# Last two key projections of dilated attention as a group of seven half-size products, two pairs of buffers for its queries and keys, and a scan begun on half of its stacks

## The reference

```python
h = rms_norm_2(x, norm_w[layer])
proj = h @ w_in[layer].astype(f32)
u_s, z_s, q, k, v, z_a, r_s, r_a = jnp.split(proj, offsets, axis=-1)
y_s = s5_branch(u_s, ...)                        # state space scan, then GLU
y_s = (y_s * jax.nn.silu(z_s)) @ w_ssm_out[layer].astype(f32)
q = apply_partial_rope(rms_norm_2(q.reshape(head_shape), q_norm_w...), positions)
k = apply_partial_rope(rms_norm_2(k.reshape(head_shape), k_norm_w...), positions)
y_a = dilated_attention(q, k, v)                 # 3 dilations, 8 heads of 64
y_a = (y_a * jax.nn.silu(z_a)) @ w_attn_out[layer].astype(f32)
m = jax.nn.sigmoid(r_s) * y_s + jax.nn.sigmoid(r_a) * y_a
x = x + m @ w_o[layer].astype(f32)
```

## Time and profile before

| what | value |
|---|---|
| three runs | 970.54, 970.54, 969.59 us, median 970.54 us |
| the profiled execution's own time | 969.14 us |
| its span, first to last instruction | 967.2 us |
| TensorE busy | 954.4 us, 99% of the span |
| VectorE busy | 697.0 us, 72% |
| ScalarE busy | 220.4 us, 23% |
| granted TensorE clock | 1.000 of full speed over the whole span |

### The profile page before, as it was taken

How to read it: one execution, slowest core, us unless ns; L and a number is a source line. 1 busy time by engine, 2 the same in 40 slices (tenths; PEclk the granted TensorE clock), 3 DMA queues, 4 the chain that set the end, 5 groups by cost and what they waited for, 6 DMA issues and landing times.

```text
span 967.2 us, 12513 instructions
## 1 busy us (share of the span) xinstructions
PE 954.4 (99%) x5014; PEld 590.6 (61%) x5014; DVE 697.0 (72%) x1259; ACT 220.4 (23%) x438; POOL 23.2 (2%) x27
## 2 busy tenths in 40 slices
PE   7999999999999999999999999999999999999998
PEld 6944445754555449999844469458854444468544
DVE  4866964586566887866899763888965969674667
ACT  4313422223241232422200011001011321434200
POOL 0000000000002500000000000000000000000000
PEclk9999999999999999999999999999999999999999
DMA  9551731443345624344454443425243434321631
GB/s 329 149 196 43 283 130 44 174 134 128 97 158 155 182 109 169 115 175 175 174 174 173 174 149 124 164 88 175 87 138 124 173 116 150 109 105 45 218 130 44
DMA packets 53818, 139.76 MB, mean 144 GB/s; under 512 B 3968, under 2 KB 7904, under 8 KB 53760
## 3 DMA queue, kind: packets, MB, share of 16 engines
q1 hardware_dynamic: 52304, 135.07, 39.7%
q0 software_dynamic: 1248, 3.80, 1.7%
q10 hardware_dynamic: 208, 0.08, 0.0%
HBM read 137.90 MB, written 1.05 MB: 144 GB/s over the span
## 4 chain that ended last, share of the span: by engine, by line
PE 92%; DVE 5%; ACT 1%; issue 1%; DMA 0%; DVEq 0%; ACTq 0%
PE pair L1947 36%; PE pair L2032 18%; PE pair L2028 16%; PE pair L2286 6%; PE turned L1892 4%; PE score L2286 3%; DVE arena L928 3%; PE turned L2286 1%; PE score L2381 1%; PE score L2457 1%; PE score L2131 1%; PE score L2444 1%; PE score L2183 1%; PE score L2130 1%; PE score L2199 1%
## 5 line engine op out<-in xcount | busy, mean ns | idle before, releaser
L1947 PE MATMUL pair<-ring,hT 128*128 128x512 f32 (+2 forms) x640 | 269.8, 576 | 0.9 <-ACT hT L600 0.9
L928 DVE TENSOR_TENSOR arena<-arena 128x512 f32<-128x512 f32 (+6 forms) x329 | 194.1, 604 | 13.4 <-PE score L2286 4.1
L1947 PEld LDWEIGHTS pair<-ring,hT 128*128 128x128 f32 x640 | 119.2, 190 | 130.5 <-issue 125.5
L1947 PE MATMUL pair<-hT,ring 128*128 128x128 f32 (+2 forms) x464 | 76.4, 324 | 0.2 <-ACT hT L600 0.2
L928 DVE TENSOR_TENSOR arena<-pair,arena 128x512 f32<-128x512 f32 x57 | 39.4, 691 | 46.6 <-PE pair L2032 22.7
L2032 PE MATMUL pair<-ring,arena 128*128 128x512 f32 x160 | 71.7, 594 | 0.0
L1947 PEld LDWEIGHTS pair<-hT,ring 128*128 128x128 f32 (+1 forms) x464 | 66.0, 188 | 9.0 <-issue 1.3
L928 DVE TENSOR_TENSOR arena<-ring 128x2048 f32<-128x2048 f32 (+1 forms) x37 | 67.7, 1831 | 2.5 <-DMA ring<-in_w_ssm_out 1.3
L2032 PE MATMUL pair<-arena 128*128 128x512 f32 x144 | 65.3, 595 | 0.3 <-DVE arena L928 0.3
L2028 PE MATMUL pair<-arena 128*128 128x128 f32 x544 | 64.0, 276 | 0.0
L2032 PE MATMUL pair<-ring,hT 128*128 128x512 f32 x136 | 62.4, 598 | 0.8 <-DMA ring<-in_w_in 0.8
(11 more groups left out here) (221 smaller groups left out, 1004.4 us busy)
## 6 DMA issues: line engine op xcount, KB each, us to landing
ring<-in_w_in SPq DMA_DIRECT2D x33, 2048.0 KB, 8.4
ring<-in_w_up SPq DMA_DIRECT2D x8, 2048.0 KB, 8.5
ring<-in_w_down SPq DMA_DIRECT2D x8, 2048.0 KB, 7.8
ring<-in_w_o SPq DMA_DIRECT2D x4, 2048.0 KB, 7.9
ring<-in_w_mem_kv SPq DMA_DIRECT2D x2, 2048.0 KB, 7.8
ring<-in_w_glu SPq DMA_DIRECT2D x2, 2048.0 KB, 7.8
ring<-in_w_ssm_out SPq DMA_DIRECT2D x2, 2048.0 KB, 7.8
ring<-in_w_ukv SPq DMA_DIRECT2D x4, 512.0 KB, 3.7
```

Source lines behind the costliest of these rows:

```text
L928: return dve.tensor_tensor(o, a, b, op)
L1947: ins = pe.matmul(o_, s, m, start=a, stop=b)
```

## The change

The blocks dk1 and dk2 become a group of seven named DK, ahead of RS. RS then shares its row sums with DK. Places for sums are moved. A second pair of buffers (`raws[1]`) is laid over memory that the scan has left; blocks alternate between the pairs. The last two blocks get one inverse root over 32 columns instead of two over 16, and their squares come from ScalarE out of SBUF after the group's results are complete. Block 5 (dk2) is turned before block 4 (dk1). Only the first eight stack copies stay on VectorE; ScalarE makes the other eight before it takes dv0. TensorE's first drive comes ahead of any quarter of the early jobs. The wait for the last transposes, which stood behind T1 of RA on VectorE, now stands ahead of it, because T1 of RA is written over a buffer that these transposes read.

```diff
@@ -81,7 +81,8 @@
 
 
 RG, MV, UP = 3, 4, 5
-RS = UP + 4
+DK = UP + 4
+RS = DK + 1
...
@@ -111,8 +112,9 @@
     j += [(f"zs{i}", "w_in_2", C_ZS + 512 * i, 512) for i in range(2)]
     j += [("za", "w_in_2", C_ZA, DW)]
     j += [(f"dq{g}", "w_in_2", C_DQ + DW * g, DW) for g in range(NDIL)]
-    j += [(f"dk{g}", "w_in_2", C_DK + DW * g, DW) for g in range(NDIL)]
+    j += [("dk0", "w_in_2", C_DK, DW)]
     out += [(n, n, w, 0, DM, c, m) for n, w, c, m in j]
+    out += halves(DK, C_DK + DW, "w_in_2")
     out += halves(RS, C_RS, "w_in_2") + halves(RA, C_RA, "w_in_2") + halves(GLU, 0, "w_glu_2")
     out += [(f"ao{i}", f"ao{i}", "w_attn_out_2", 0, DW, 512 * i, 512) for i in range(2)]
...
 
...
         assert a4.at <= work_at
+        raws = ((raw, raw2), (sig_glu[:, 0:1024], sig_glu[:, 1024:2048]))
         tail_q1, tail_q5 = arena[:, 7680:8192], arena[:, 16384:16896]
-        tail_t2 = {RS: m_tok, RA: sig_glu, GLU: m_tok, SO: arena[:, work_at:work_at + 2048], WP: arena[:, work_at + 4096:work_at + 6144]}
+        tail_t2 = {DK: arena[:, 0:2048], RS: arena[:, 2048:4096], RA: sig_glu, GLU: zs, SO: arena[:, work_at:work_at + 2048], WP: arena[:, work_at + 4096:work_at + 6144]}
         rows_raw = arena[:, work_at + 6144:work_at + 8192]
-        tail_rows = {RS: zs, RA: zs, GLU: rows_raw, SO: arena[:, work_at + 2048:work_at + 4096], WP: rows_raw}
+        tail_rows = {DK: m_tok, RS: m_tok, RA: m_tok, GLU: rows_raw, SO: arena[:, work_at + 2048:work_at + 4096], WP: rows_raw}
...
@@ -443,6 +448,18 @@
 
             t, g = n // 2, 2 * (i - UP) + n % 2
             return hup[:, 1024 * g:1024 * g + 1024].rearrange("p (k t) -> p k t", t=SEQ)[:, :, P * t:P * t + P]
+
+        def stacks(i):
+
+            u4 = uT.rearrange("p (m c s) -> p m c s", c=CH, s=2)
+            v4 = u2.rearrange("p (m h c) -> p m h c", h=2, c=CH)
+            out_ = []
+            for h in range(2):
+                for jj in range(2):
+                    for s in range(2):
+                        q, r = 64 * h + 32 * jj, 64 * jj + 32 * s
+                        out_.append((h, jj, s, u4[q:q + 32, 4 * i:4 * i + 4, :, s], v4[r:r + 32, 4 * i:4 * i + 4, h, :]))
+            return out_
 
         block = ctx.enter_context(nc.Block())
...
@@ -816,6 +833,10 @@
                     if t == 0:
                         ins.then_inc(sem("u_ready"), 1)
                 ins.then_inc(sem("taken_act"), 1)
+            act.wait_ge(sem("taken_act"), taken("us1")[1])
+            for h, jj, s, src, dst in stacks(1):
+                ins = act.activation(dst, src, ACT.Copy)
+            ins.then_inc(sem("u2_late"), 1)
...
-                if n:
-                    for _k in range(2):
-                        turned((qdT if n - 1 < 3 else kdT)[:, 1024 * ((n - 1) % 3) + 512 * _k:1024 * ((n - 1) % 3) + 512 * _k + 512], 512)
-                if n == 0:
-                    act.wait_ge(sem("h_ready"), 4 * 8)
+            def turned_dqk(n):
+
+                for k in range(2):
+                    turned((qdT if n < 3 else kdT)[:, 1024 * (n % 3) + 512 * k:1024 * (n % 3) + 512 * k + 512], 512)
+
+            act.wait_ge(sem("z_silu"), 3)
+            act.wait_ge(sem("h_ready"), 4 * 8)
+            for n, name in enumerate(("dq0", "dq1", "dq2", "dk0")):
+                x, squares = raws[n % 2]
                 p = arrived(name)
                 for t in range(2):
-                    act.activation(raw[:, 512 * t:512 * t + 512], p[:, 512 * t:512 * t + 512], ACT.Copy)
+                    act.activation(x[:, 512 * t:512 * t + 512], p[:, 512 * t:512 * t + 512], ACT.Copy)
                 for t in range(2):
-                    ins = act.activation(raw2[:, 512 * t:512 * t + 512], p[:, 512 * t:512 * t + 512], ACT.Square)
+                    ins = act.activation(squares[:, 512 * t:512 * t + 512], p[:, 512 * t:512 * t + 512], ACT.Square)
                 ins.then_inc(sem("taken_act"), 1)
-                if n == 2:
+                if n == 0:
                     for i in range(2):
                         act.wait_ge(sem("gelu_z"), i + 1)
                         act.activation(gz[:, 1024 * i:1024 * i + 1024], gz[:, 1024 * i:1024 * i + 1024], ACT.Sigmoid,
                                        scale=1.5957691216057308).then_inc(sem("gelu_sig"), 1)
+                else:
+                    turned_dqk(n - 1)
+            group_copy(DK, 1)
+            group_copy(DK, 5)
+            turned_dqk(3)
+            group_first(DK, raws[1][0][:, 0:512])
+            act.wait_ge(sem("first_out"), DK + 1)
+            act.wait_ge(sem("second_out"), DK + 1)
+            act.activation(raws[0][1], raws[0][0], ACT.Square).then_inc(sem("dk_squared"), 1)
+            act.wait_ge(sem("group_act"), act_at(DK, 3))
+            act.wait_ge(sem("last_out"), DK + 1)
...
@@ -983,15 +1017,15 @@
 
                 _, _, (b11, b12, _, _), _, (t2, _) = group(i)
                 weights_in(f"g{i}x")
-                if i and i != RA:
-                    dve.wait_ge(sem("group_product"), product_at(i - 1 if i != GLU else RS, 6))
+                if 0 < i < DK or i in (SO, WP):
+                    dve.wait_ge(sem("group_product"), product_at(i - 1, 6))
                 mark(tt(t2, b11, b12, ALU.add), "group_sums")
 
             def group_t3(i):
 
                 _, _, (_, b12, _, b22), _, (_, t3) = group(i)
                 weights_in(f"g{i}y")
-                if 0 < i < RS:
+                if 0 < i < DK:
                     dve.wait_ge(sem("group_product"), product_at(i - 1, 7))
                 mark(tt(t3, b12, b22, ALU.add), "group_sums")
 
...
+
+                if n < 4:
+                    dve.wait_ge(sem("taken_act"), taken(("dq0", "dq1", "dq2", "dk0")[n])[1])
+                else:
+                    dve.wait_ge(sem("dk_squared"), 6 - n)
+                link(dve.tensor_reduce(st[:, at:at + 16], squares.rearrange("p (g c) -> p g c", c=DD), AX.X, ALU.add))
+
+            def dqk_turn(n, x, scratch, at):
...
-            u4 = uT.rearrange("p (m c s) -> p m c s", c=CH, s=2)
-            v4 = u2.rearrange("p (m h c) -> p m h c", h=2, c=CH)
...
+            def dqk(n):
+
+                x, squares = raws[n % 2]
+                dqk_squares(n, squares, 192)
+                mean(st[:, 192:208], st[:, 192:208], DD)
+                inverse_root(192, 16)
+                dqk_turn(n, x, squares, 208)
+
+            dve.wait_ge(sem("taken_act"), taken("us0")[1])
+            for h, jj, s, src, dst in stacks(0):
+                ins = dve.tensor_copy(dst, src)
+                step(ins) if (h, jj, s) != (1, 1, 1) else mark(ins, "u2_ready")
 
...
-            dqk(0)
             ssm_out(7)
-            dqk(1)
             for i in range(2):
                 y, z = uT[:, 1024 * i:1024 * i + 1024], gz[:, 1024 * i:1024 * i + 1024]
                 link(tt(z, y, y, ALU.mult))
                 link(dve.tensor_scalar(z, z, 0.044715, 1.0, ALU.mult, ALU.add))
                 mark(tt(z, z, y, ALU.mult), "gelu_z")
-            dqk(2)
+            dqk(0)
+            group_rows(DK)
             for i in range(2):
                 dve.wait_ge(sem("gelu_sig"), i + 1)
                 y, z = uT[:, 1024 * i:1024 * i + 1024], gz[:, 1024 * i:1024 * i + 1024]
                 mark(tt(y, y, z, ALU.mult), "gelu_ready")
                 link(tt(z, y, zs[:, 1024 * i:1024 * i + 1024], ALU.mult))
-            group_rows(RS)
+            dqk(1)
+            group_t1(DK)
+            dqk(2)
+            group_t3(DK)
             dqk(3)
+            group_t2(DK)
+            group_t4(DK)
             group_t1(RS)
-            dqk(4)
+            group_z(DK)
+            group_middle(DK, raws[0][0][:, 0:512], raws[0][0][:, 512:1024])
+            group_last(DK, raws[1][0][:, 512:1024])
             group_t3(RS)
-            dqk(5)
+            dqk_squares(5, raws[0][1], 192)
+            dqk_squares(4, raws[1][1], 208)
+            mean(st[:, 192:224], st[:, 192:224], DD)
+            inverse_root(192, 32)
+            dqk_turn(5, raws[0][0], raws[0][1], 224)
             group_t2(RS)
+            dqk_turn(4, raws[1][0], raws[1][1], 240)
             group_t4(RS)
             group_z(RS)
+            dve.wait_ge(sem("turned_ready"), T_DQK)
             group_t1(RA)
-            dve.wait_ge(sem("turned_ready"), T_DQK)
             group_rows(GLU)
             rs4, ra4, glu4 = by_tokens(rsig), by_tokens(asig), by_channels(sig_glu)
             group_middle(RS, rs4[1], rs4[3])
@@ -2388,18 +2438,20 @@
             pe.wait_ge(sem("turned_taken"), n_unit["turned"])
             pe.wait_ge(sem("m0_taken"), 1)
             pe.wait_ge(sem("ca_ready"), 2)
-            fill(early, 0, 2)
             for m in range(8):
-                if m in (0, 4):
-                    pe.wait_ge(sem("u2_ready"), m // 4 + 1)
+                if m == 0:
+                    pe.wait_ge(sem("u2_ready"), 1)
+                if m == 4:
+                    pe.wait_ge(sem("u2_late"), 1)
                 drive(m)
-                fill(early, 3 * m + 2, 1)
```

(75 more changed lines are left out.)

5 lines of the change are left out of this document (1 added, 4 removed).

## The result

| | median us | runs | granted clock |
|---|---|---|---|
| before | 969.88 | 969.08 to 970.54 (11) | 1.000 in the profiled run |
| after | 973.81 | 971.08 to 975.73 (11) | 0.994 to 0.998 in every run |

The ratio is 1.0039, 95% interval 1.0028 to 1.0049: slower by 3.8 us. (The ratios in this document compare the means of all runs of two kernels, each with those of the kernel before that ran beside it.) The forecast was 1.75 us slower, 972.3. The profiled execution took 974.35 us (before 969.14), its span is 972.5 (967.2).

The account below looks back on a forecast made before the run. TensorE, busy 99%, bounds the kernel; its 3.43 us gain is lost to waits for a VectorE late at the scores, plus 1.75 us: 970.54 + 1.75 = 972.3 us. Forecast 971.3 to 973.1, stated range 970.0 to 974.3.

Parts of the forecast that it names:

- TensorE's gain: dk1 and dk2, two jobs of 27.47 us, become seven products of 24.04 us: 3.43 us less if hidden entirely.
- The scan's earlier start: First drive ahead of the early jobs: 0 us for TensorE by itself; VectorE starts scanning 7 us earlier.
- rival D: Earlier scan brings VectorE nothing; gelu delays dqk(0) by up to 3 us, inside the 3.8 margin: sum unchanged; chance 0.01.
- VectorE up to the group: VectorE's work from dq0 to z at 782.8: all in time for TensorE, margins 1.1 to 4.6 us.
- The root over 32 columns: Mean and root on VectorE for the last two blocks, ahead of block 5's turn: taken at 2.5 us.
- Where it tips: VectorE full from 791.11, scores at 823.85 instead of 822.10; TensorE waits 2.4 and 3.5 us, ending 1.75 us later.
- The shift stays to the end: Attention rounds behind the scores are led by TensorE's list, so the 1.75 us shift stays to the end.
- rival C: Clock falls in the new waits of 2.4 and 3.5 us: some 1.8 us on top, 974.1 us; chance 0.06.
- B: Rival: VectorE later still, at z or block 5, stalling RS's last products: 1.3 to 3 us more, 973.6 to 975.3; chance 0.16.
- the paragraph on the clock: At the kernel's start TensorE ran at about half speed, losing some 1.8 us; the skill's rule speaks against both new waits.

Follow-up runs that it names:

- VectorE's list cut: Work not yet due (T3 of RA, GLU's row sums) moved behind the scores on VectorE: changed kernel 966.88 us, 0.9965; kernel before, without the group, 969.86 us, 0.9995.
- the late VectorE: Kernel before plus two useless VectorE operations (2.33 us each) ahead of the scores: 976.29 us, ratio 1.0067.
- the fed waits: Changed kernel plus five useless matmuls in TensorE's two new waits: 971.89 us, ratio 1.0018.
- the best kernel: Changed kernel with T3 of RA and GLU's row sums moved behind the scores, RS's v and two blocks ahead of the last transposes' wait: 966.88 us, ratio 0.9965.

## Why the prediction was right, and where it was short

The sign, the place of the waits and the mechanism by which VectorE's list eats the gain were right; half of the slowdown was not in the sum. *TensorE's gain*: 3.43 us was the sum; 0.9965 with the group and 0.9995 without it, both with VectorE's list cut, are 2.9 us apart, with 1.4 and 0.8 us of interval to either side of them, and the two traces are 3.43 apart. *The scan's earlier start*, worth nothing to TensorE by itself: shown (164.0 us against 164.1). I gave what it buys as gelu's room ahead of dq0, and took it for a detail: rival D says that gelu ahead of dqk(0) delays it by up to 3 us, inside the margin of 3.8. That is refuted. With the early scan undone the delay is 6.5 us (730.44 - 723.97), TensorE waits twice, and it costs 1.5 us. *VectorE up to the group*: no wait up to 818, as said; all margins held. *The root over 32 columns* was taken at 2.5 us and took 2.46 (from 797.13, where its first operation starts, to 799.59, where the turn of block 5 follows).

*Where it tips*: the scores on VectorE were forecast for 823.85 and came at 824.36, which is 823.9 without the 0.46 us of scatter; the first wait was forecast at 2.4 us and was 2.39. The second was to be 3.5 us and was 2.79, because the half-product ahead of it took 2.46 us in place of the 1.98 of the earlier trace rows (the clock had already fallen) and I had counted it some 0.15 us too short. *The shift stays to the end*: shown by the late VectorE and by the fed waits.

The forecast itself claimed 971.3 to 973.1, and 973.81 lies outside. The stated range holds it only because it was stretched over rival C and half of B; the time is within 0.3 us of C's 974.1, to which I gave 0.06. That part is luck, the more so as the price in C came from the start of the kernel. There 20 records take 0.20 us each, but the granted clock of that stretch is 1.00, and 0.50 stands only behind the waits:

```profile
5.00:8.00 3.00, 2.75 (x13) 2.75 (x14) 1.26 (x10) 2.30 (x4) 0.00 (x0) 1.00 1.03 352
```

So the profile does not confirm that those records were slow by the clock.

The step that failed is the size of the whole, in the paragraph on the clock. I had the two waits, their lengths and the row at the start of the kernel, and still left the clock out of the sum, with a chance of 0.06 and a price of 1.8 us. It fell in all 11 runs. The price was 3.0 us in the profiled execution and 2.0 us over all runs (1.0039 against 1.0018 with the waits filled). My argument against it, that a half-product lies between the two waits, is what the runs refute: TensorE was idle for 5.2 of the 7.6 us between 818.3 and 825.9, and the half-product in between already ran slow towards its end. Before's own 0.48 us and 0.45 us waits, and those of 0.48 and 0.71 us in the fed kernel, left it at 1.00.

The Trainium skill ("TensorE: Matmul & The Clock Gate", HAM oscillation) says that long gaps in the matmul stream cost twice, by the wait and by the half clock behind it. The trace agrees in kind: waits of 2.39 and 2.79 us there were followed by 3.0 us of lost clock. I cited the rule and did not put it into the sum.

## What to carry to other kernels

Where one engine is busy 99% and its products are traded for sums on another, lay the second engine's list beside the first up to the next point where they meet: here 3.4 us saved became 1.75 us lost, by sums of which 5.2 us (T3 of RA and GLU's rows) were not yet due. Once a list shows that TensorE will wait for 2 to 3 us or more, put the lower clock behind the wait into the sum; here it cost 2 to 3 us. And before undoing such a change, move what is not due behind the meeting point, in pieces that fit the gaps there: the same saving then came out whole in the trace (3.43 us), and as 2.9 us over the runs.

## What the runs showed of the hardware

A single wait of 2.81 us lowered the clock in 6 of 12 runs of one kernel, waits of 2.39 and 2.79 us close together in all 11, of 2.39 and 1.82 us (the scan's part undone) in all 5, one of 5.14 us in all 6, and waits up to 0.92 us in none of the 5 of the best kernel. (The lengths are those of the profiled execution; the other runs have only their clock and time.) The loss differs from run to run: the changed kernel ranges over 4.7 us, the fed one over 1.6 us. The kernel before shows a clock of 0.998 now and then as well, in 2 of 29 runs beside the first experiments, at 972.0 and 972.1 us where the others have a median of 969.9, and in 1 of 21 beside the later ones, at 971.2. The trace of before is of a run at 1.000, and behind its first 20 us no wait of TensorE is above 0.8 us; what lowers the clock in those other runs is open.
